# Turning the experts' rows on VectorE instead of TensorE, with quarter-row gathers, 16 KB weight runs and a later down projection

## What is computed

```python
def hier_moe(h, prm):
    ...            # best of 4 groups, then the best two of its 4 experts, for each token
    y = zeros
    for e in range(16):                       # rows = the tokens that chose e
        a = silu(h[rows] @ w_gate[e]) * (h[rows] @ w_up[e])       # w_gate, w_up: 1024 x 512
        y[rows] += weight[rows] * (a @ w_down[e])                 # w_down: 512 x 1024
    return y
...
x = x + hier_moe(rmsnorm(x))
y = rmsnorm_final(x)
```

## Time and profile before

| | us |
|---|---|
| three runs of the kernel | 1175.77, 1178.63, 1184.39 |
| median | 1178.63 |
| span of the profiled execution (first to last instruction) | 1175.0 |

### The profile page before, as it was taken

The page is one execution under the profiler, slowest core; times in us unless marked ns, Lnnn a source line. Parts: engine busy times, 40 slices in busy tenths (PEclk is TensorE's granted clock), DMA queues, the critical chain, the costliest instruction groups (busy, mean ns, idle before and its releaser), DMA issues.

```text
span 1175.0 us, 23400 instructions
## 1 busy us (share of the span) xinstructions
PE 1112.4 (95%) x10096; PEld 780.1 (66%) x10096; DVE 462.6 (39%) x924; ACT 373.6 (32%) x844; POOL 259.8 (22%) x152
## 2 busy tenths in 40 slices
PE   5999999999999988888899999899999999999995
PEld 3666666666666667867644554387788877888784
DVE  3200566548765666687644322620100001111034
ACT  4110545454334365764622211111111110111152
POOL 0000000001110179999800000121111112111102
PEclk8999999999999989999999999889999999999998
DMA  6611100001100310002053741188989889998994
GB/s 204 163 37 36 59 18 19 19 18 41 40 24 18 45 28 4 4 4 56 6 199 94 269 165 72 59 286 284 325 309 304 306 298 318 333 313 278 324 385 163
DMA packets 95683, 174.06 MB, mean 148 GB/s; under 512 B 19988, under 2 KB 41175, under 8 KB 95172
## 3 DMA queue, kind: packets, MB, share of 16 engines
q1 hardware_dynamic: 88372, 151.92, 37.3%
q0 software_dynamic: 7200, 20.57, 6.6%
HBM read 147.45 MB, written 27.75 MB: 149 GB/s over the span
## 4 chain that ended last, share of the span: by engine, by line
PE 85%; DVE 9%; ACT 2%; issue 2%; SPq 0%; DMA 0%; POOLq 0%; POOL 0%; DVEq 0%; ACTq 0%
PE ps L776 23%; PE ps L1496 20%; PE ps L1294 10%; PE ps L1519 9%; PE ps L1525 1%; PE ps L855 1%; PE ps L879 1%; PE ps L868 1%; PE ps L1472 1%; PE ps L1046 1%; DVE arena L2320 1%; PE ps L1005 1%; ACT arena L2047 1%; PE ps L1145 1%; PE ps L1374 1%
## 5 line engine op out<-in xcount | busy, mean ns | idle before, releaser
L776 PE MATMUL ps<-arena 128*128 128x352 f32 (+1 forms) x960 | 297.6, 466 | 2.8 <-issue 2.6
L1496 PEld LDWEIGHTS ps<-arena 128*128 128x128 f32 x2048 | 245.9, 191 | 7.8 <-issue 6.1
L776 PEld LDWEIGHTS ps<-arena 128*128 128x128 f32 x960 | 180.3, 191 | 106.4 <-issue 11.4
L1496 PE MATMUL ps<-arena 128*128 128x128 f32 (+4 forms) x2048 | 248.3, 283 | 0.7 <-ACT arena L2022 0.6
L1294 PE MATMUL ps<-arena 128*128 128x512 f32 x256 | 116.4, 597 | 0.7 <-DVE arena L2405 0.7
L1519 PE MATMUL ps<-arena 128*128 128x512 f32 x256 | 113.3, 595 | 0.7 <-DVE arena L2680 0.7
L2030 ACT ACTIVATE arena<-ps 128x128 f32<-128x128 f32 (+4 forms) x64 | 18.3, 285 | 278.5 <-PE ps L1496 278.5
L2680 DVE TENSOR_TENSOR arena<-arena,ps 128x128 f32<-128x128 f32 (+4 forms) x64 | 19.1, 299 | 212.8 <-ACT arena L2030 212.8
L1519 PEld LDWEIGHTS ps<-arena 128*128 128x128 f32 x256 | 47.4, 190 | 55.1 <-issue 53.6
L2864 POOL TENSOR_TENSOR arena<-arena 128x1024 f32<-128x1024 f32 x4 | 11.4, 2857 | 320.4 <-DVE arena L2206 320.4
L1294 PEld LDWEIGHTS ps<-arena 128*128 128x128 f32 x256 | 46.8, 190 | 52.8 <-issue 51.0
(11 more groups left out here) (422 smaller groups left out, 1552.7 us busy)
## 6 DMA issues: line engine op xcount, KB each, us to landing
arena<-in_w_exp_gate SPq DMA_DIRECT2D x16, 2048.0 KB, 11.0
arena<-in_w_exp_up SPq DMA_DIRECT2D x16, 2048.0 KB, 16.0
arena<-in_w_exp_down SPq DMA_DIRECT2D x16, 2048.0 KB, 15.6
arena<-in_w_in SPq DMA_DIRECT2D x16, 512.0 KB, 3.8
arena<-in_x_prompt SPq DMA_DIRECT2D x9, 512.0 KB, 4.3
x_dram<-arena SPq DMA_DIRECT2D x9, 512.0 KB, 3.6
h_dram<-arena SPq DMA_DIRECT2D x8, 512.0 KB, 2.6
out_y_prompt<-arena SPq DMA_DIRECT2D x8, 512.0 KB, 3.4
```

The costliest lines, as they stand in the source:

```text
L776: last = pe.matmul(ps[:, q % 2, 0:m], wr[:, n % 3, k, :], hT[:, k, a:a + m], start=(k == 0), stop=(k == KB - 1))
L1496: last = pe.matmul(ps[:, 3 + f % 2, n * CAP:n * CAP + CAPS[e]], w[a][:, k, f * P:(f + 1) * P], xgT[:, a, k, 0:CAPS[e]], start=(k == 0), st ...
```

## The change

Experts 1 to 15 are no longer turned by PE.

- Gathers: POOL gathers the 128 rows as 4 x 128 quarter rows of 1 KB by a new table of indices `idxG`, so that DVE's 32x32 transposes, 4 an expert and 1 more for a tail, write `xgT` directly (L2674 of the new kernel). They stand between the second and third product of the expert before and signal `xt_ok`. Expert 0 still goes through PE, ACT and DVE as before. `idxG` costs 16 small matmuls in place of one ahead of `idxB`; the old one, needed for the weights, stands behind.
- Weights: since a DVE transpose leaves row `8p+b` of the inner dimension on partition p, the weights are loaded as `(p b)`: one run of 16 KB a partition. For down that takes every fourth column of the inner width together, so the stationary block f of gate and up is `f::4`, 128 columns at a step of 16 bytes. The gate and up of expert 0 keep the old layout of their rows.
- Order: `down(e-1)` stands behind block 0 of `gate_up(e)` instead of ahead of it, on PE, and so do the evictions on ACT and DVE. On DVE the first product of expert 15 stands ahead of `own`, `sums` and the `bulk`s, and the second behind the first six `bulk`s.

```diff
-                sp.dma_start(dst[a], src.rearrange("(b p) f -> p b f", p=P))...
+                sp.dma_start(dst[a], src.rearrange("(b p) f -> p b f" if whole and n < 2 else "(p b) f -> p b f", p=P))...
...
-            def turn(r, e, between=lambda: None):
...
-                        last = pe.transpose(ps[:, j, k * P:(k + 1) * P], xgA[:, a, (4 * j + k) * P:(4 * j + k + 1) * P], ident)
...
+            def gate_up_ready(r, e, later):
+                a = e % 2
+                if e or later:
+                    pe.wait_ge(s["xt_ok"], NE * r + e)
...
+                pe.wait_ge(s[f"w{a}"], WBASE[a] + 32 * (NE // 2 * r + e // 2 + 1))
...
-                            last = pe.matmul(ps[:, 3 + f % 2, n * CAP:n * CAP + CAPS[e]], w[a][:, k, f * P:(f + 1) * P], xgT[:, a, k, 0:CAPS[e]],
+                        last = pe.matmul(ps[:, 3 + f % 2, n * CAP:n * CAP + CAPS[e]], w[a][:, k, f::FF // P], xgT[:, a, k, 0:CAPS[e]],
...
-                pe.matmul(ps[:, 7, 0:2 * NE], slots[:, 0:P], st_["stackP"], start=True, stop=True).then_inc(s["hot_ps"], 1)
+                for b in range(P // XB):
+                    for j in range(TQ):
+                        last = pe.matmul(ps[j * XB:(j + 1) * XB, 0, b * NE:(b + 1) * NE], slots[:, b * XB:(b + 1) * XB], st_["stackP"][:, 0:NE],
+                                         start=True, stop=True, tile_position=(0, j * XB))
+                last.then_inc(s["hot_ps"], 1)
...
-                for e in range(1, NE - 2):
-                    turn(r, e)
-                    down(r, e - 1)
-                    gate_up(r, e)
...
+                for e in range(NE):
+                    gate_up_ready(r, e, later)
+                    gate_up(r, e, 0)
+                    if e:
+                        down(r, e - 1)
+                    for f in range(1, 4):
+                        gate_up(r, e, f)
                 down(r, NE - 1)
...
+        LANES = "p (c k) -> p k c"
...
+            def turn_block(a, src, b):
+                return dve.transpose(xgT[:, a, :, b * XB:(b + 1) * XB], src.rearrange(LANES, k=KB))
...
+            def turn(r, e):
+                a = e % 2
+                dve.wait_ge(s[f"xg{a}"], gathered(r, e))
+                if e != 1 or not isinstance(r, int):
+                    dve.wait_ge(s["gu_ps"], 4 * (NE * r + e - 1))
+                for b in range(P // XB):
+                    last = turn_block(a, xgA[:, a, b * TD:(b + 1) * TD], b)
+                if TAIL[e]:
+                    dve.wait_ge(s[f"xq{a}"], ...)
+                    last = turn_block(a, xgQ[:, a, :], P // XB)
+                last.then_inc(s["xt_ok"], 1)
...
                 for e in range(NE - 1):
-                    turned(r, e)
+                    product(g0 + e, e, 0)
                     if 0 < e <= ACC:
                         rows_out(r, e - 1)
...
-                    product(g0 + e, e)
+                    product(g0 + e, e, 1)
+                    turn(r, e + 1)
+                    for f in range(2, 4):
+                        product(g0 + e, e, f)
...
-                product(g0 + NE - 1, NE - 1, after_last)
+                after_last(0)
+                for f in range(1, 4):
+                    product(g0 + NE - 1, NE - 1, f)
+                    after_last(f)
...
-                    gather(xgA[:, e % 2, :], h2_dram, idxF[:, 0:1] if early else idxA[:, e:e + 1])...
+                        for b in range(P // XB):
+                            gather(xgA[:, e % 2, b * TD:(b + 1) * TD], h2_quarters, idxG[:, b, e:e + 1])...
```

More of the change, by code:

```diff
@@ L305, in program @@
         smpA = sb("smpA", [P, LAST], I32)
-        STEPS = 7 + 2 + 4
+        STEPS = 8 + 2 + 4
         OUT = [0, 1, 2, NT] + list(range(3, NT))
@@ L1461, in _, with turn_first @@
             fill(512)
[L1464 to L1467 removed]
+            def turn_first():
+                pe.wait_ge(s["xg0"], 16)
                 for j in range(2):
[L1469 to L1470 removed]
                     for k in range(4):
[L1472 removed]
+                        last = pe.transpose(ps[:, j, k * P:(k + 1) * P], xgA[:, 0, (4 * j + k) * P:(4 * j + k + 1) * P], ident)
@@ L1483, in turn @@
[L1483 to L1489, removed]
-                pe.wait_ge(s[f"w{a}"], WBASE[a] + 32 * (NE // 2 * r + e // 2 + 1))
[L1491 to L1495, removed]
-                            last = pe.matmul(ps[:, 3 + f % 2, n * CAP:n * CAP + CAPS[e]], w[a][:, k, f * P:(f + 1) * P], xgT[:, a, k, 0:CAPS[e]],
-                                             start=(k == 0), stop=(k == KB - 1))
-                    last.then_inc(s["gu_ps"], 1)
+                if TAIL[0]:
+                    pe.wait_ge(s["r_dve"], 8)
+                    pe.wait_ge(s["xq0"], 16)
+                    for c in range(TD // P):
+                        last = pe.transpose(ps[:, 2, c * P:(c + 1) * P], xgQ[:, 0, c * P:(c + 1) * P], ident)
+                    last.then_inc(s["xb_ps"], 1)
@@ new lines, in gate_up_ready, with gate_up @@
+            def gate_up_ready(r, e, later):
+                a = e % 2
+                if e or later:
+                    pe.wait_ge(s["xt_ok"], NE * r + e)
+                    alone(pe)
+                else:
+                    pe.wait_ge(s["xa_ok"], 2)
+                    pe.wait_ge(s["xb_ok"], 1)
+                pe.wait_ge(s[f"w{a}"], WBASE[a] + 32 * (NE // 2 * r + e // 2 + 1))
+            def gate_up(r, e, f):
+                g, a = NE * r + e, e % 2
+                if not (e == 0 and f < 2):
+                    pe.wait_ge(s["ac_ok"], 4 * g + (f - 1))
+                for n, w in enumerate((egate, eup)):
+                    for k in range(KB):
+                        last = pe.matmul(ps[:, 3 + f % 2, n * CAP:n * CAP + CAPS[e]], w[a][:, k, f::FF // P], xgT[:, a, k, 0:CAPS[e]],
+                                         start=(k == 0), stop=(k == KB - 1))
+                last.then_inc(s["gu_ps"], 1)
@@ L1552, in one_round @@
                 last.then_inc(s["hot_ps"], 1)
+                pe.matmul(ps[:, 7, 0:2 * NE], slots[:, 0:P], st_["stackP"], start=True, stop=True).then_inc(s["hot_ps"], 1)
                 if not later:
@@ L1562, in one_round @@
                 if not later:
[L1563 to L1566, removed]
-                for e in range(1, NE - 2):
-                    turn(r, e)
-                    down(r, e - 1)
-                    gate_up(r, e)
[L1572 to L1577, removed]
+                    turn_first()
+                for e in range(NE):
[5 more added lines that the diff above has]
+                        gate_up(r, e, f)
                 down(r, NE - 1)
@@ L2016, in _, with first_turned_in, silu @@
             act.copy(slotsF, ps[:, 5, 0:CAP]).then_inc(s["r_act"], 1)
-            def turned(g, a):
+            def first_turned_in():
                 for j in range(2):
[L2021 to L2031, removed]
+                    act.wait_ge(s["xa_ps"], j + 1)
+                    act.copy(xgT[:, 0, 4 * j:4 * j + 4, 0:P], ps[:, j, :].rearrange("p (k c) -> p k c", k=4)).then_inc(s["xa_ok"], 1)
+            def silu(g, e, f):
+                c = CAPS[e]
+                act.wait_ge(s["gu_ps"], 4 * g + (f + 1))
+                if not (e == 0 and f < 2):
+                    act.wait_ge(s["ac_ok"], 4 * g + (f - 1))
+                act.activation(egl[:, f % 2, 0:c], ps[:, 3 + f % 2, 0:c], ACT.Silu).then_inc(s["sl_ok"], 1)
             def rows_out(r, e):
@@ L2088, in at_last @@
                         table(ACT.Sqrt, 54)
+                if not later:
+                    first_turned_in()
                 for e in range(NE):
-                    turned(g0 + e, e % 2)
+                    silu(g0 + e, e, 0)
                     if 0 < e <= ACC:
                         rows_out(r, e - 1)
[L2094 to L2097, removed]
+                    for f in range(4):
+                        if f:
+                            silu(g0 + e, e, f)
+                        if e == NE - 2:
+                            before_last(f)
+                        elif e == NE - 1:
+                            at_last(f)
                 act.wait_ge(s["h2o0"], H2O[0] + 16 * 5 * (r + 1))
@@ L2809, in after_last @@
                         own(eyA[:, 0, :], 1, 34)
+                if later:
+                    turn(r, 0)
+                else:
+                    first_tail_turned()
+                    rounds_needed()
                 for e in range(NE - 1):
-                    turned(r, e)
-                    if not (e or later):
-                        rounds_needed()
+                    product(g0 + e, e, 0)
                     if 0 < e <= ACC:
```

70 lines of the change are left out of this document (36 added, 34 removed).

## The result

The changed kernel takes 1397.63 us (median of four runs, 1395.59 to 1402.75) beside 1181.51 us before in the same comparison: a ratio of 1.1842, with an interval of 1.1799 to 1.1885. It is 18% slower. The forecast was 1177.3 us in a range of 1161 to 1260; the measured time is 138 us above the range.

What follows compares the result with a forecast made beforehand. PE, busy 95% of the span, was taken as the bound. Terms -14.8 + 1.1 + 8.0 + 2.5 + 1.9 = -1.3 us from 1175.0 gave 1173.7, plus 3.6 for the median: 1177.3 us, range 1161 to 1260.

Steps and rivals of the forecast that it cites:

- The strided stationary operand: Gate and up on PE: loading every fourth column costs nothing; 180 us kept as the end, called the largest unknown.
- 69 ns of slack: Gate and up's load at 128 columns was put at 44 ns, far below a pass of 113.
- DVE's pair of rows: DVE reductions of 128x144: 403 ns at a step of four floats, 304 without; 0.69 ns more an element.
- the rival of slow loads: Rival 1: loads of every fourth column lengthen gate and up passes by 25 to 180 us; 1265 us, chance 0.23.
- Stall ahead of expert 15: At the end PE waits for expert 15's late weights, because of the later down: +8.0 us (6 to 10).
- Clock behind it: After the stall PE's granted clock may fall to 0.50: +2.5 us (0 to 10).
- DVE's order at the end: Expert 15's products wait behind `own`, `sums` and `bulk`s on DVE: +1.9 us (0 to 4).
- Index step: Sixteen small matmuls for four on PE, at half the granted clock: +1.1 us.
- DVE's transposes: Between products of blocks 1 and 2, 0.40 to 0.58 us each, 0.58 taken; they fit and cost nothing.
- POOL: Four gather issues instead of one for 15 experts, 3 us more in mostly waiting time; nothing taken, 0 to 1 us.
- the transposes as 14.8 us of PE's time: Removing PE's transposes for experts 1 to 15 and eight tails counts whole: -14.8 us.
- the later down as a cost alone: Down behind gate and up's first block shrinks the weights' cover to 5 us and costs at the end.

Runs made afterwards that it cites:

- the ladder above: Changed kernel with gate and up's stationary operand at steps of 8, 12 and 32 bytes instead of 16: 1181.11, 1280.38 and 1404.31 us, one run each.
- the run with neighbouring columns: Changed kernel with 128 neighbouring columns stationary again and down back in runs of 4 KB; 1177.21 us, 0.9959 of the time before.
- The run with down first at all experts: Run with neighbouring columns, but down again ahead of gate and up's first block for experts 1 to 15; 1181.58 us, 1.0008 of before.

## Why the prediction was wrong

**The step that failed** is "The strided stationary operand", "I take nothing, because it is another engine and the load has 69 ns of slack by those rows". Measured it is 232 us: a load takes 232 ns, 119 above the pass of 113, and sets the pace at every number of rows. Neither half of the reason held. Another engine was no reason: PE pays for the step as DVE does, and more. Since a load of neighbours hides in a pass of 113 ns, the step adds at least 119 ns to it, 0.93 ns an element, where DVE's pair of rows had 0.69. And the slack, read as 69 ns from records at 32 and 128 columns, was no cover. How large it is no run shows, since a load of neighbours stays behind the matmul; by the estimate of 58 ns it is 55 ns, and the step adds 174. Even the upper end, 88 ns on each pass, 180 us, was too low, because I took DVE's price as the largest.

The Trainium skill's rule ("Advanced Engine Details and Errata", section "SBUF Cachelines") had named the mechanism: lines of 16 bytes, two hits on each to hide the access, a penalty for a new one at each value. The runs agree on the penalty: at a step of 8 bytes, two hits a line, a pass costs 6 ns more, at 16 bytes 119. That two hits hide the whole access they do not show: by the ladder above a line costs the same with one hit as with two. I gave the rival of slow loads 0.23, and a time of 1265 us; its mechanism was right, with the gap at the end gone as it said, and its size, about 100 us, less than half of the 232.

**The terms beside it were right in kind**, which the run with neighbouring columns shows. That it took 1177.21 us beside the sum's 1177.3 is luck: its ratio, 0.9959, is 4.8 us below before, where the sum has 1.3. Term by term:

- Stall ahead of expert 15: 8.0 forecast, 7.8 measured. The chain from `down(12)` over the added rows to the weights is the one that I counted.
- Clock behind it: 2.5 forecast, as the middle of 0 and 5; 1.9 measured, because the clock was at half for about 4 us and not for 10. That the two are near is luck.
- DVE's order at the end: 1.9 forecast, 0.8 measured. With it the terms as measured, -14.8 + 0.9 + 7.8 + 1.9 + 0.8, make -3.4 us, beside -4.4 between the medians.
- Index step: 1.1 forecast, 0.9 measured. DVE's transposes: 0.58 us each forecast, as the most, 0.613 measured, and PE waited for none. POOL: nothing, and PE's waits show nothing.
- In the changed kernel itself the end costs nothing, since slow passes give the weights time: its PE never waited for weights.

**One working was right in its sum and wrong in its reasons.** I counted the transposes as 14.8 us of PE's time and the later down as a cost alone. The run with down first at all experts shows that the transposes were also the cover for silu and product, and that the 14.8 us are there only with the later down. What comes late when a stretch of work goes, I asked of DVE, POOL and the weights, but not of the product right behind.

## What to carry to other kernels

Before a layout is chosen for the sake of longer transfer runs, look at what it does to the step of PE's operands: here 128 float32 values took 1.8 ns for each line of 16 bytes touched, so a step of 16 doubled the passes, on the stationary and on the moving side, while a step of 8 was nearly free (tried on the stationary side alone). An unknown of that size, in a group that is a fifth of the span, deserves a kernel of its own before the whole. And when work is taken off the engine that bounds the kernel, ask what its time covered: put other ready work in its place, but not where the last experts' loads hang on it.

## What was not expected of the hardware

- The price of a load follows lines of 16 bytes, not steps: 119, 175, 232 and 237 ns at 8, 12, 16 and 32 bytes.
- A pass of PE whose load is the bound has records that show it: the matmul's mean was the same, 397 ns, from 128 to 160 columns. With the moving operand as the bound it rose from 407 to 463.
- Longer runs did little for the transfers: packets on the queue that carries the weights fell from 88372 before to 61492 with neighbouring columns, but their time from 37.3% of 1175 us, 438 us, to 36.4% of 1179.1, 429 us. The pages of the two:

```profile
q1 hardware_dynamic: 88372, 151.92, 37.3%
```

```profile
q1 hardware_dynamic: 61492, 151.92, 36.4%
```
